# Latent attention heads in pairs, totals spread by TensorE, and scores, maximum and exponential ahead of the linear part in each step

## What is computed

```python
def block_causal_attention(q, k, v):          # 8 heads, q and k of 64 + 32 (rope), v of 64
    def one_block(args):                      # blocks of 128 queries
        s = jnp.einsum('bqhd,bkhd->bhqk', q_blk, k) * scale
        s = jnp.where(k_chunk[None, :] <= qc[:, None], s, finfo.min)   # chunks of 64
        p = jax.nn.softmax(s, axis=-1)
        return jnp.einsum('bhqk,bkhe->bqhe', p, v)

q_mla = concat([qh[..., :64], q_pe]);  k_mla = concat([kvh[..., :64], k_pe for every head])
o_gla  = rms_norm(gla_chunked(g_q, g_k, g_v, log_a)) * silu(gate)
o_ret  = rms_norm(retention_chunked(r_q, r_k, rv)) * silu(gate)
return concat([o_mla, o_gla, o_ret]) @ w_out
```

## Time and profile before

| | us |
|---|---|
| median of 3 runs | 1942.91 |
| lowest and highest | 1942.43, 1943.5 |
| the profiled execution, whole time | 1942.39 |
| its span in the profile | 1940.6 |

### The profile page before, as it was taken

One profiled execution on the slowest core, in us unless ns is written; L12 is line 12 of the kernel. 1 busy time (PEld: TensorE's weight loads), 2 busy tenths in 40 slices (PEclk: granted clock), 3 DMA queues, 4 the chain that ended last, 5 costly groups with the idle time before them and its releaser, 6 DMA issues.

```text
span 1940.6 us, 31226 instructions
## 1 busy us (share of the span) xinstructions
PE 1908.9 (98%) x12792; PEld 1711.4 (88%) x12792; DVE 1225.4 (63%) x1631; ACT 792.0 (41%) x1148; POOL 637.2 (33%) x490
## 2 busy tenths in 40 slices
PE   7999999999999999999999999999999999999998
PEld 6999988897668999998899999889966789999886
DVE  5888843534555788872578888344354467888523
ACT  5344433334454444442443444232344544444322
POOL 3566500002230566620045664000022325666000
PEclk9999999999999999999999999999999999999999
DMA  4233233321003123323312333332200122222321
GB/s 164 88 109 108 103 121 125 102 100 44 1 23 130 46 108 108 108 109 131 130 44 88 108 108 109 130 131 95 86 22 3 64 87 88 106 93 105 127 101 66
DMA packets 27370, 180.43 MB, mean 93 GB/s; under 512 B 3298, under 2 KB 3460, under 8 KB 7300
## 3 DMA queue, kind: packets, MB, share of 16 engines
q1 hardware_dynamic: 25760, 174.15, 25.1%
q10 hardware_dynamic: 1508, 4.87, 0.8%
HBM read 176.91 MB, written 2.10 MB: 92 GB/s over the span
## 4 chain that ended last, share of the span: by engine, by line
PE 95%; ACT 1%; DVE 1%; issue 1%; DMA 0%; SPq 0%; POOLq 0%; POOL 0%; DVEq 0%; ACTq 0%
PE ps L461 27%; PE ps L463 27%; PE ps L462 27%; PE ps L811 2%; PE ps L700 1%; PE ps L829 1%; PE ps L473 1%; PE ps L621 1%; PE ps L623 1%; PE ps L622 1%; PE ps L709 1%; PE ps L818 1%; PE ps L762 0%; PE ps L756 0%; DMA raw<-stream 0%
## 5 line engine op out<-in xcount | busy, mean ns | idle before, releaser
L461 PE MATMUL ps<-xH,WH 128*128 128x256 f32 (+2 forms) x1424 | 427.5, 300 | 3.0 <-DVE xL L1314 3.0
L463 PE MATMUL ps<-xH,WL 128*128 128x256 f32 (+2 forms) x1424 | 424.9, 298 | 0.0
L462 PE MATMUL ps<-xL,WH 128*128 128x256 f32 (+2 forms) x1424 | 424.9, 298 | 0.0
L462 PE MATMUL ps<-TL,WH 128*128 128x256 f32 x1216 | 344.5, 283 | 0.0
L463 PE MATMUL ps<-TH,WL 128*128 128x256 f32 x1216 | 344.5, 283 | 0.0
L461 PE MATMUL ps<-TH,WH 128*128 128x256 f32 x1216 | 344.5, 283 | 0.0
L1265 DVE TENSOR_TENSOR WL<-raw,WH 128x2048 fp32r<-128x2048 f32 x62 | 143.0, 2307 | 264.4 <-ACT WH L925 249.5
L461 PEld LDWEIGHTS ps<-xH,WH 128*128 128x128 f32 (+1 forms) x1424 | 273.4, 192 | 11.8 <-issue 4.3
L462 PEld LDWEIGHTS ps<-xL,WH 128*128 128x128 f32 (+1 forms) x1424 | 273.3, 192 | 8.5 <-issue 1.0
L463 PEld LDWEIGHTS ps<-xH,WL 128*128 128x128 f32 (+1 forms) x1424 | 273.3, 192 | 7.6
L461 PEld LDWEIGHTS ps<-TH,WH 128*128 128x128 f32 x1216 | 233.6, 192 | 0.0
(11 more groups left out here) (249 smaller groups left out, 3655.1 us busy)
## 6 DMA issues: line engine op xcount, KB each, us to landing
raw<-stream SPq DMA_DIRECT2D x156, 1024.0 KB, 4.8
norm_g<-norm_gains SPq DMA_DIRECT2D x12, 512.0 KB, 5.3
x<-x_in SPq DMA_DIRECT2D x4, 512.0 KB, 8.1
wq<-w_q_up ACTq DMA_DIRECT2D x4, 512.0 KB
out<-x SPq DMA_DIRECT2D x4, 512.0 KB, 2.7
const<-consts ACTq DMA_DIRECT2D x2, 578.5 KB
wkv<-w_kv_up ACTq DMA_DIRECT2D x2, 512.0 KB
cos<-positions ACTq DMA_DIRECT2D x2, 256.0 KB
```

Of the source, the lines that this page charges most:

```text
L461: mm(dst, wh, xh, start=start, stop=False)
L462: mm(dst, wh, xl, start=False, stop=False)
L463: return mm(dst, wl, xh, start=False, stop=stop)
```

## The change

Latent heads are taken in pairs. A step is still one head and one block, but the two heads of a pair alternate: steps 0 to 7 are blocks 0 to 3 of heads 0 and 1. Even and odd heads keep their plain and rotated rows in opposite halves of the bank, so one product makes the keys of both heads with all 128 rows. Four buffers each hold queries and keys, three the turned probabilities.

Values are made for both heads of a block at once, every second step, with v as weights (64 wide) and the turned probabilities as 128 columns; one head's output lands in rows 0 to 63 of the bank and the other's in rows 64 to 127, already with tokens along the columns. So the output isn't turned any more. The reciprocal totals are spread over the bank by eight products with the identity (`spread_shares`), ACT keeps them (`keep_shares`), DVE multiplies once for a pair (`scale_heads`), ACT keeps the high part, and POOL makes the low part (`low_heads`).

Queries of a pair are made in steps 0 and 4 of the pair before, its keys in step 2, the spread is in step 6. turn_q waits for keep_q. The copies of the rotated key rows for the third and fourth key buffers are made by ACT in steps 1 and 3.

In each step scores stand ahead of linear on PE, exps ahead of linear on ACT, and tops ahead of linear on DVE. The order of the first and last output tiles is `[1, 6, 2]` and `[3, 4, 5, 0, 7]`.

```diff
+def head_and_block(m):
+    return m // 8 * 2 + m % 2, m % 8 // 2
...
+                    def make_k(i):
+
+                        pe.wait_ge(q_kept, due(q_kept, 2 * i + 1))
+                        pe.wait_ge(q_ready, due(q_ready, 2 * i + 1))
+                        mm(ps[:, QK_BANK, :], wkv[:, 2 * i * NOPE:(2 * i + 2) * NOPE],
+                           ckv[:], start=True, stop=True).then_inc(k_psum, 1)
...
+                        if m >= 4:
+                            pe.wait_ge(turn_kept, due(turn_kept, m - 3))
...
+                    def values(p):
+                        h, b = head_and_block(2 * p)
+                        pe.wait_ge(turn_kept, due(turn_kept, 2 * p + 2))
...
                         for kk in range(b + 1):
-                            last = mm(ps[:, OUT_BANK, b * DV:(b + 1) * DV], probT[:, m % 2, kk * P:(kk + 1) * P],
-                                      v_mla[:, kk, h * DV:(h + 1) * DV], start=kk == 0, stop=kk == b)
+                            for e in range(2):
+                                last = mm(ps[e * DV:(e + 1) * DV, OUT_BANK, b * P:(b + 1) * P],
+                                          v_mla[:, kk, (h + e) * DV:(h + e + 1) * DV],
+                                          p_of[(2 * p + e) % 3][:, kk * P:(kk + 1) * P], start=kk == 0, stop=kk == b)
                         last.then_inc(valued, 1)
+
+                    def spread_shares(i):
+
+                        pe.wait_ge(share_ready, due(share_ready, i + 1))
...
+                        for b in range(BLK):
+                            for e in range(2):
+                                at = 2 * b + e
+                                last = mm(ps[e * DV:(e + 1) * DV, QK_BANK, b * P:(b + 1) * P],
+                                          share[:].rearrange("p a b -> p (a b)")[:, at:at + 1].broadcast_to([P, DV]),
+                                          ident[:], start=True, stop=True)
+                        last.then_inc(share_spread, 1)
...
                     for n in range(STEPS):
-                        h, b = divmod(n, BLK)
+                        i = n // 8 + 1
                         turn(n)
-                        if n:
-                            values(n - 1)
-                        if h + 2 < HEADS and b == 1:
-                            make_q(h + 2)
-                        if h + 2 < HEADS and b == 2:
-                            make_k(h + 2)
-                        if h and h % 2 == 0 and b == 3:
-
-                            turn_heads(h // 2 - 1, QK_BANK)
-                        linear(n)
+                        if n and n % 2 == 0:
+                            values(n // 2 - 1)
+                        if i < HEADS // 2:
+                            if n % 8 == 0:
+                                make_q(2 * i)
+                            elif n % 8 == 2:
+                                make_k(i)
+                            elif n % 8 == 4:
+                                make_q(2 * i + 1)
+                        if n % 8 == 6:
+                            spread_shares(i - 1)
                         if n + AHEAD < STEPS:
                             scores(n + AHEAD)
-                        else:
+                        linear(n)
...
                     for n in range(STEPS):
-                        h, b = divmod(n, BLK)
+                        i = n // 8 + 1
                         keep_turn(n)
...
+                        if n + AHEAD < STEPS:
+                            exps(n + AHEAD)
                         linear(n)
                         if n == NORM_STEP + 2:
                             high_at(base, 9)
-                        if n + AHEAD < STEPS:
-                            exps(n + AHEAD)
...
                     for n in range(STEPS):
-                        h, b = divmod(n, BLK)
-                        if h and b == 0:
-                            keep_head(h - 1)
-                        if b == 2:
-                            shares(h)
-                        if h and h % 2 == 0 and b == 3:
-                            low_heads(h // 2 - 1, QK_BANK)
-                        if h + 2 < HEADS and b == 1:
-                            turn_q(h + 2)
-                        linear(n)
+                        i = n // 8 + 1
+                        if n and n % 8 == 0:
+                            scale_heads(i - 2)
+                        if i < HEADS // 2 and n % 8 in (0, 4):
+                            turn_q(2 * i + n % 8 // 4)
                         if n + AHEAD < STEPS:
                             tops(n + AHEAD)
+                        linear(n)
+                        if n % 8 == 5:
+                            invert_totals(i - 1)
...
+                def low_heads(i):
+
+                    pool.wait_ge(headsH_ready, due(headsH_ready, i + 1))
+                    nc.gpsimd.tensor_tensor(xL[:, i, :], head_out, xH[:, i, :].bitcast(F32),
+                                            ALU.subtract).then_inc(headsL_ready, 1)
```

More of the change, by code:

```diff
@@ L81 @@
 SPLITS = FT // 2
-MIX_START, MIX_REST = [0, 1, 6], [2, 3, 4, 5, 7]
+MIX_START, MIX_REST = [1, 6, 2], [3, 4, 5, 0, 7]
 TWO_PI = 6.283185307179586
@@ L260, in hybrid_trunk @@
         sign = const[:, C_SIGN:C_SIGN + 1]
-        twice = const[:, C_TWICE:C_TWICE + 2 * ROPE]
+        twice = const[:, C_TWICE:C_TWICE + P]
         head_sel = const[:, C_HSEL:C_HSEL + 2]
         inv_freq = const[:, C_INV:C_INV + 1]
-        pair_out = (kt_gla, kt_ret)
+        q_of = (qT[:, 0, :], qT[:, 1, :], acc[:], q_spare[:])
+        k_of = (kT[:, 0, :], kT[:, 1, :], sin[:], zg[:])
+        head_share, head_out = (t[:].rearrange("p b f -> p (b f)") for t in (kt_gla, kt_ret))
+        p_of = (probT[:, 0, :], probT[:, 1, :], ks_ret[:])
         further = {3: W3, 4: W4, 5: W5}
@@ L1212, in mixer @@
                     for j in range(2):
-                        af(kT[NOPE:P, j, :], ps[NOPE:P, LIN_BANKS[0], :], ACT.Copy).then_inc(kpe_copied, 1)
+                        r = rope_rows(j)
+                        af(k_of[j][r, :], ps[r, LIN_BANKS[0], :], ACT.Copy).then_inc(kpe_copied, 1)
                     keep_k(0)
@@ L1221, in mixer @@
                     for n in range(STEPS):
-                        h, b = divmod(n, BLK)
+                        i = n // 8 + 1
                         keep_turn(n)
-                        if h and h % 2 == 0 and b == 3:
-                            keep_heads(h // 2 - 1, QK_BANK)
-                        if h + 2 < HEADS and b == 1:
-                            keep_q(h + 2)
-                        if h + 2 < HEADS and b == 2:
-                            keep_k(h + 2)
+                        if n > 8 and n % 8 == 1:
+                            keep_heads(i - 2)
+                        if n % 8 == 6:
+                            keep_shares(i - 1)
+                        if i < HEADS // 2:
+                            if n % 8 == 0:
+                                keep_q(2 * i)
+                            elif n % 8 == 2:
+                                keep_k(i)
+                            elif n % 8 == 4:
+                                keep_q(2 * i + 1)
+                        if n in (1, 3):
+                            j = n // 2
+                            r = rope_rows(j)
+                            act.wait_ge(kpe_copied, due(kpe_copied, j + 1))
+                            af(k_of[j + 2][r, :], k_of[j][r, :], ACT.Copy).then_inc(kpe_copied, 1)
+                        if n + AHEAD < STEPS:
+                            exps(n + AHEAD)
                         linear(n)
@@ L1814, in _ @@
                 low_gated(3)
+                low_heads(2)
+                low_heads(3)
                 ffn(3 * layer + 2, 2 * layer + 1, first_pair_of(3 * layer + 2))
```

192 lines of the change are left out of this document (106 added, 86 removed).

## The result

The changed kernel takes 1948.24 us (median of 6 runs, 1946.66 to 1949.62), the kernel before 1942.67 (median of 6 that ran beside them, 1939.81 to 1943.88). The ratio is 1.0033 with a 95% interval of 1.0024 to 1.0043: slower, by 5.6 us. That lies in the stated range of 1932 to 1950, but not where I put the forecast, 1943 and no difference. It is the sign of rival 2, and near its 1950.

The account below looks back on a forecast made before the run. PE, busy 98% of the span, was taken to bound the kernel. Per layer, -8.7 us of work, +9.1 of waits and -0.3 of clock gave +0.1, +0.2 for two layers: 1943 us, range 1932 to 1950.

Parts of the forecast that it names:

- rival 2: Clock falls at new waits in steps 1, 5 and 13: +6.8 us in all, 1950 us; chance 0.18.
- What bounds the kernel: PE, busy 98% of the span; ACT and DVE cost only latency, where PE waits for their chains.
- the walk through the queues: Instructions of PE, ACT and DVE placed in their new order: 12.8 us of idle PE a layer against 3.7.
- -8.7 of PE work: PE work a layer: values -6.9, K -4.2, the heads' turn replaced by spreads +2.3; together -8.7 us.
- +9.1 of idle: PE's waits a layer after the reordering: 12.8 us where the same stretch had 3.7, so +9.1.
- the form change: PE's switch to 64-row products and back: 0.08 us each, counted inside the group prices, 20 more a layer.
- rival 3: Array halves don't overlap in values: +6.9 us a layer, 13.8 in all, 1957 us; chance 0.04.
- The clock: Lower clock around the squares, taken as 1.7 us a layer and expected unchanged, some 0.3 falling in existing waits.
- The forecast's case: Whole kernel: work saved and new waits cancel, 1943 us, between the lines at 1939 and 1947; chance 0.44.
- Other edits: Cos product, turn_q's wait for keep_q, kpe copies, POOL's low parts: covered; the wait moves make_k(0) by 0.5 us.
- The tail: After the last values: 4.4 us of helper work covered by five down tiles of 1.4 us each; pair 11 loads earlier.

Follow-up runs that it names:

- e4: Changed kernel with two more products of 512 columns, result unused, in step 13 between scores and retention_scores; 1948.84 us.
- e5: Changed kernel with the squares' products given 128 moving columns instead of 2; 1944.8 us.
- e6: Kernel before with the squares' products given 128 moving columns instead of 2 and nothing else; 1940.47 us, ratio 0.999.
- e7: Changed kernel with the linear part first on all three engines, and queries, keys and spread moved to odd steps; 1936.66 us, ratio 0.9976 to the kernel before.
- e9: e7 with squares' products of 128 moving columns and, in the same way, wide products for the latents' norms; 1936.72 us.
- e2: Kernel before, heads one by one, with only scores, exps and tops put ahead of the linear part on PE, ACT and DVE; 1945.64 us, ratio 1.0017.

## Why the prediction came out as it did

**What bounds the kernel, and the walk through the queues: right.** The list of waits came out nearly as written. Expected and measured in us: scores(1) 1.4 and 1.28, turn(0) 0.2 and 0.21, state_parts(2) 1.8 and 1.53, linear_values(0) 1.3 and 1.13, retention_scores in step 7 1.2 and 1.00, in step 13 2.6 and 2.55, the squares 0.3 and 0.47, values(9) 0.6 and 0.60, values(12) 1.4 and 1.24, scores(30) 0.6 and 0.37. Only the 0.5 at gated_scores(0) and the 0.4 in step 10 hardly showed. The chain of step 13 is there as it was told, keep_q, turn_q, maximum, exponential, gated copies, keep_low, and then PE (start, us, engine; changed kernel):

```profile
531.69 0.59 ACT L1183 ACTIVATE qT<-ps 64x512 f32<-64x512 f32 x1 [2.00 <-PE ps L720]
...
532.42 0.68 DVE L1615 TENSOR_TENSOR qT<-ps,cos 64x512 f32<-64x512 f32 x1 [5.16 <-ACT qT L1183]
...
533.26 0.69 DVE L1699 TENSOR_REDUCE top<-ps 128x1 f32<-128x512 f32 x1
...
534.17 0.69 ACT L1202 ACTIVATE prob<-ps,minus_top 128x512 f32<-128x512 f32 x1 [1.89 <-DVE minus_top L1700]
...
534.85 0.76 ACT L1237 ACTIVATE attn_g<-ps 64x256 f32<-64x256 f32 x2
...
535.74 0.89 DVE L1644 COPY_PREDICATED attn_g<-const,ps 64x256 f32<-64x256 int32 x2 [1.61 <-ACT attn_g L1237]
...
536.78 0.89 PE L764 MATMUL ps<-qx,heads 128*64 128x256 f32 x4 [2.55 <-DVE attn_g L1644]
```

The DVE row for turn_q names the step that carried most: DVE stood idle 5.16 us, until ACT's copy.

**The sums of work and of waits: both too large, by nearly the same amount.** I had -8.7 of PE work and +9.1 of idle a layer. Measured idle is 11.2 against 4.4, so +6.8; with 0.7 left over, PE saved 6.1. That the two errors of 2.6 and 2.3 cancel is luck. Idle was over-stated by small things: most of the waits came out 0.1 to 0.3 short, and the hop from one engine to the next is mostly at the lower end of my 0.1 to 0.25. The work term failed at the form change. I had put its 0.08 into the price of the groups, but it is paid on the product in front as well (changed kernel; start, us):

```profile
510.97 0.66 PE L843 MATMUL ps<-ident,prob 128*128 128x128 f32 x4
511.46 0.60 PE L836 MATMUL ps<-sin,acc 128*128 128x256 f32 x2
...
513.64 0.33 PE L843 MATMUL ps<-ident,prob 128*128 128x128 f32 x1
513.90 1.09 PE L855 MATMUL ps<-probT,v_mla 128*64 128x128 f32 x16
514.92 1.99 PE L720 MATMUL ps<-mq,wq 128*128 128x512 f32 x4
...
519.79 0.33 PE L843 MATMUL ps<-ident,prob 128*128 128x128 f32 x1
519.96 0.81 PE L836 MATMUL ps<-sin,acc 128*128 128x384 f32 x2
```

One transpose takes 0.26 us from its start to the next when values follow and 0.17 when scores do; with four it is 0.59 (507.27 to 507.86) against the 0.49 above. Sixteen groups a layer make about 1.5 us; small groups of values, at 0.37 for two products instead of 0.33, and K at 0.97 make most of the rest. The Trainium skill (TensorEngine Tiling (Array Packing), Key Properties) says that a change of the tiling mode drains TensorE; the trace agrees, with about 0.1 us on the way in besides the 0.08 that I had. Values of 8 products took 1.02 us, as the row of linear_spread said, so rival 3 is out.

**The clock: this is the step that failed.** "The squares stay and come closer together, so I expect the same loss." One interval a layer was taken over; there were two or three, 4 to 5 us over the runs. The reason against rival 2 was wrong: waits of up to 1.2 us without a fall said nothing of one of 2.55 us right behind 0.7 us of small products. I had the row of the squares itself, where the clock fell behind 1.75 us of little work, and my own walk showed a wait longer than that. It should have been the forecast. Rival 2 had the mechanism and its sign, but not its places: of the waits in steps 1, 5 and 13 only that in step 13 was followed by the lower clock in the changed kernel, in both layers; the third interval of the first layer came behind values(12) and scores(30), and it isn't in the profiles of e4 and e5 with the same waits. So the length of a wait alone doesn't tell whether the clock falls behind it. What the price depends on I also had only in part: e4 shows that the fall moves to the next thin place when one is filled, and e5 and e6 that the squares cost either kernel some 2 to 3 us, so that they carry little of the difference.

**The sign.** At full clock the change is 1.3 us slower, which is the forecast of no difference (+0.2) within its error, by the luck of the two sums; the clock makes it 5.6. The forecast's case held 0.44 and that of the clock 0.18, and it is the second that came. It lies inside the range only because the range was drawn out to rival 2's 1950.

**Other edits.** The wait of turn_q for keep_q I named, and gave it 0.5 us under cover and its part in scores(1). Its price as an edit by itself was never worked out, though it stands in four of my chains. It is 8.3 us in the changed kernel: without it the change would have been a gain of 2.9. That rival, faster than before by one wait less, was not among mine. The tail (down tiles, POOL's low parts, pair 11) cost nothing, as said: the tiles follow each other at 0.68 to 0.70 us for three products from 591.7 us on.

## What to carry to other kernels

When work is moved ahead or made thinner on a full engine, list its instructions between each producer and the one that waits for its result: the thinnest such gap, not the mean load, sets the new waits. Spreading fillers evenly (e7) gave 7.0 us, over half of the 12 us of PE work that the pairs save in two layers. Price each added wait by itself, through everything queued behind it on its engine: 0.59 us in one queue was 5 us of waits over two layers. And where PE's waits grow to the length of a thin place at which the clock already falls, count the lower clock as part of the price. Before a remedy is credited with a loss, try it in the kernel before as well (e6): what it gives there was no part of the loss.

## What the runs showed of the hardware

Products of 2 moving columns and of 128, on weights of 128 by 128 in float32, take nearly the same time (1.70 and 1.78 us for eight), but a kernel with the wide ones keeps the higher of the two clock levels more often: 3.4 us less in one kernel, 2.0 in another. In e9 they gave nothing over e7. The clock also makes most of the run-to-run spread where that is wide: e2's ten runs lie between 1942.8 and 1953.8 us with mean clocks of 0.997 and 0.990. In the kernel before it doesn't: runs with a mean clock of 0.996 lie between 1939.2 and 1944.3 us. And the best version here, pairs with the linear part first, fillers in the odd steps, wide products and a free turn_q, takes 1928.83 us against 1943.08 of the kernel before beside it, 14 us less.
